# A fused two-block network on one core: GpSimd takes the lower halves of sixteen weight tiles

## What is computed

```
mod   = (silu(c)     @ w_mod[l] + b_mod[l])
mod_c = (silu(c_ctx) @ w_mod[l] + b_mod[l])
...
hc = modulate(ctx_s, g_norm1[l], csh1, csc1)
zc = hc @ w_in[l]
qc, kc, vc = qkv_heads(zc, g_q[l], g_k[l])
...
yc_attn = gqa(qc, kc, vc)
yc_conv, yc_four = local_branches(zc, w_conv[l])
ctx_s = ctx_s + cgt1 * merge_branches(zc, yc_conv, yc_four, yc_attn, ...)
```

## Time and profile before

| what | value |
|---|---|
| median of 3 runs | 3247.83 us (3245.22 to 3250.43) |
| the profiled execution | 3244.21 us |
| its span in the trace | 3242.4 us |
| mean granted TensorE clock | 0.991 of full speed |
| context attention with its 52 tiles | about 89 to 224 us of the span |

### The profile page before, as it was taken

One profiled execution on the slowest core, in us unless ns is written; L12 is line 12 of the kernel. 1 busy time (PEld: TensorE's weight loads), 2 busy tenths in 40 slices (PEclk: granted clock), 3 DMA queues, 4 the chain that ended last, 5 costly groups with the idle time before them and its releaser, 6 DMA issues.

```text
span 3242.4 us, 42575 instructions
## 1 busy us (share of the span) xinstructions
PE 3180.1 (98%) x16062; PEld 2675.1 (83%) x16062; DVE 2084.7 (64%) x2904; ACT 1232.2 (38%) x1792; POOL 0.2 (0%) x4
## 2 busy tenths in 40 slices
PE   8899999999999999999999999999999999999998
PEld 6889998887888888888788888887888878888886
DVE  6777886665687777656475565875544676664446
ACT  4664445454232223554332222535222266542221
POOL 0000000000000000000000000000000000000000
PEclk9999999999999999999999999999999999999999
DMA  7654552212344553311222322222222336223232
GB/s 272 202 187 158 179 190 85 72 53 72 110 137 140 175 186 104 104 52 53 82 88 91 103 97 97 79 97 78 98 97 96 106 72 88 69 78 104 98 97 72
DMA packets 100715, 358.17 MB, mean 110 GB/s; under 512 B 11208, under 2 KB 12368, under 8 KB 100560
## 3 DMA queue, kind: packets, MB, share of 16 engines
q1 hardware_dynamic: 98864, 352.85, 32.8%
q10 hardware_dynamic: 1696, 3.16, 2.1%
HBM read 351.76 MB, written 2.10 MB: 109 GB/s over the span
## 4 chain that ended last, share of the span: by engine, by line
PE 90%; DVE 5%; ACT 2%; issue 1%; DMA 0%; DVEq 0%; ACTq 0%; SPq 0%
PE ring L1689 26%; PE ring L1690 25%; PE ring L1691 25%; PE bank L1689 2%; PE bank L1691 2%; PE bank L1690 2%; DVE w_lo L2580 1%; ACT w_hi L898 1%; PE ring L2015 1%; PE ring L2016 1%; PE bank L2040 1%; PE bank L2041 1%; PE ring L1986 1%; DVE x L3340 0%; PE bank L2171 0%
## 5 line engine op out<-in xcount | busy, mean ns | idle before, releaser
L1689 PE MATMUL ring<-h_hi,w_hi 128*128 128x512 f32 (+1 forms) x2776 | 1027.2, 370 | 18.2 <-DVE h_lo L2651 8.4
L1690 PE MATMUL ring<-h_lo,w_hi 128*128 128x512 f32 (+1 forms) x2776 | 1019.2, 367 | 0.0
L1691 PE MATMUL ring<-h_hi,w_lo 128*128 128x512 f32 (+1 forms) x2776 | 1019.0, 367 | 0.0
L2580 DVE TENSOR_TENSOR w_lo<-raw,w_hi 128x1024 fp32r<-128x1024 f32 x598 | 730.9, 1224 | 306.6 <-ACT w_hi L898 293.9
L898 ACT ACTIVATE w_hi<-raw 128x1024 fp32r<-128x1024 f32 x598 | 630.5, 1056 | 707.5 <-PE ring L1691 667.7
L1689 PEld LDWEIGHTS ring<-h_hi,w_hi 128*128 128x128 f32 x2776 | 528.7, 190 | 111.4 <-issue 16.3
L1691 PEld LDWEIGHTS ring<-h_hi,w_lo 128*128 128x128 f32 x2776 | 528.1, 190 | 86.1
L1690 PEld LDWEIGHTS ring<-h_lo,w_hi 128*128 128x128 f32 x2776 | 528.7, 190 | 82.3
L1689 PE MATMUL ring<-y_hi,w_hi 128*128 128x512 f32 (+1 forms) x1456 | 540.2, 371 | 11.5 <-DVE z L2870 7.8
L1691 PE MATMUL ring<-y_hi,w_lo 128*128 128x512 f32 (+1 forms) x1456 | 536.4, 368 | 0.0
L1690 PE MATMUL ring<-y_lo,w_hi 128*128 128x512 f32 (+1 forms) x1456 | 536.2, 368 | 0.0
(11 more groups left out here) (381 smaller groups left out, 3075.1 us busy)
## 6 DMA issues: line engine op xcount, KB each, us to landing
raw<-ws SPq DMA_DIRECT2D x606, 512.0 KB, 3.3
z<-ws SPq DMA_DIRECT2D x52, 512.0 KB, 4.5
x<-ws SPq DMA_DIRECT2D x4, 512.0 KB, 9.5
x<-x_t SPq DMA_DIRECT2D x1, 2048.0 KB, 10.9
out_t<-x SPq DMA_DIRECT2D x8, 256.0 KB, 2.0
z<-xc ACTq DMA_DIRECT2D x6, 256.0 KB, 11.3
xc<-ctx_t SPq DMA_DIRECT2D x1, 1024.0 KB, 12.4
z<-ropes ACTq DMA_DIRECT2D x2, 512.0 KB, 4.0
```

The source lines that it names most:

```text
L1689: nc.tensor.matmul(o, a_hi, b_hi, start=start, stop=False)
L1690: nc.tensor.matmul(o, a_hi, b_lo, start=False, stop=False)
L1691: return nc.tensor.matmul(o, a_lo, b_hi, start=False, stop=stop)
L2580: nc.vector.tensor_tensor(w_lo[:, u, :], raw[:, u, :], f(w_hi[:, u, :]), ALU.subtract).then_inc(w_ready, 1)
```

## The change

The lower part of every second modulation tile (odd index i, the second of each pair) of this attention is computed by GpSimd: 16 tiles, numbers 2, 5, 8, 11, 15, 18, 21, 24, 28, 31, 34, 37, 41, 44, 47 and 50. GpSimd waits for `w_hi_ready` of the tile, subtracts, and raises its own count `s_pool_low`. GpSimd does not raise `w_ready`. VectorE does that: when it comes to its next call of `lower_w`, it first waits for its own earlier tiles, then for GpSimd, and raises `w_ready` by one; then it makes the tile of that call. The loads, ScalarE's queue and TensorE's queue are unchanged.

```diff
+POOL_MODS = (1,)
...
+        pool_tiles = [at0 + n for kind, layer, stream, at0 in steps if (kind, layer, stream) == ("attn", 0, "ctx")
+                      for n, (of, i) in enumerate(fill_tiles(layer, stream)) if of == "mod" and i % 2 in POOL_MODS]
...
+        @block.gpsimd
+        def _(pool):
+            for n, t in enumerate(pool_tiles):
+                pool.wait_ge(w_hi_ready, t + 1)
+                nc.gpsimd.tensor_tensor(w_lo[:, t % R, :], raw[:, t % R, :], w_hi[:, t % R, :].bitcast(F32), ALU.subtract)\
+                    .then_inc(s_pool_low, 1)
...
+            pool_read = [0]
+
             def lower_w(c, off=0):
 
                 t = c + LEAD
                 if isinstance(off, int) and t >= n_tiles:
+                    return
+                while pool_read[0] < len(pool_tiles) and pool_tiles[pool_read[0]] < t:
+                    dve.wait_ge(w_ready, pool_tiles[pool_read[0]])
+                    pool_read[0] += 1
+                    dve.wait_ge(s_pool_low, pool_read[0])
+                    dve.sem_inc(w_ready, 1)
+                if t in pool_tiles:
                     return
```

More of the change, by code:

```diff
@@ L588, in build @@
         s_chunk_sum = sem("mod_products_summed")
+        s_pool_low = sem("w_lo_ready_by_pool")
         s_out = sem("stored")
```

## The result

The changed kernel takes 3253.1 us (median of 20 runs, 3250.2 to 3256.7), the kernel before 3247.5 us in the same rounds: a ratio of 1.0018, 95% interval 1.0012 to 1.0025. One of the 20 executions of the kernel before took 16463 us and is left out of the ratio. The changed kernel is slower by 5.6 us, where +2 was forecast and +7.5 was the price of the rival in which GpSimd and VectorE shut each other out. The time lies in the range given and inside the band called "same", near its upper end.

A forecast was written before the change was run, and what follows sets the result against it. TensorE, busy 98%, was taken to bound the kernel, VectorE counting only where TensorE waits for it. Terms +1.5 + 1.3 + 1.3 - 2.15 gave +2 us on 3247.8: 3250 us, range 3244 to 3258 us.

The forecast's parts named there:

- the case in which the engines run side by side: Context attention: GpSimd and VectorE work without blocking each other; +2 us, 3250 us, 48% chance.
- the shut-out: Rival: GpSimd's subtraction and VectorE's operations on two local-memory operands cannot run together; +7.5 us, 3255 us, 25% chance.
- What bounds the kernel: Context attention: TensorE is busy 98% of the span; freeing VectorE is worth only TensorE's waits for it, 11.7 us.
- d = 2.45 us: GpSimd's time for one subtraction of 1024 columns, taken as twice VectorE's 1.226 us.
- The relief, -2.15 us: Tiles 15, 28 and 41, directly before branch reads: reads come earlier by 0.45, 1.0 and 0.7 us.
- the rival of the relief: Rival: TensorE's waits at three branches go, 5.6 us, plus 1.5 us of half clock; -7 us, 3241 us, 10% chance.
- The first chain, +1.5 us: Tiles 8 and 9, before the query parts and TensorE's longest single wait: 1.3 us later, plus hand-overs.
- The second chain, +1.3 us: Tile 50, before the load of tile 54 and TensorE's last wait: 1.1 us later, plus the hand-over.
- The other ten pairs, +1.3 us: Remaining odd tiles and the tiles behind them: mostly covered, 1.3 us together, mostly at tiles 21 to 25.
- my three terms: The added delays at tiles 8 and 9, at tile 50 and at the other ten pairs: +1.5, +1.3 and +1.3 us.
- the rival with a slow GpSimd: Rival: a GpSimd subtraction takes near 4.9 us or starts several us late; some +17 us, 3265 us, 7% chance.
- the half clock forecast at 151 to 157 us: Changed profile: a stretch of half clock there would speak for GpSimd and VectorE excluding each other.

The follow-up runs named there:

- e7: Changed kernel with all 16 lower parts left out, made by nobody, VectorE passing readiness on itself: 3242.5 us, 0.9986 of the kernel before.
- e12: Changed kernel with only the lower parts of tiles 15, 28 and 41 left out and GpSimd doing nothing: 3242.4 us, 0.9987 of the kernel before.
- e2: Changed kernel with tiles 8 and 50 back on VectorE, so GpSimd makes 14: 3252.3 us, 1.0020 of the kernel before.
- e3: Changed kernel with GpSimd filling the 16 lower parts with zeros twice (2.0 us) instead of subtracting, all waits kept: 3244.8 us, 0.9996 of the kernel before.
- e10: Changed kernel with GpSimd filling the 16 lower parts with zeros three times (3.0 us) instead of subtracting, waits kept: 3252.4 us, 1.0013 of the kernel before.
- e8: The changed kernel unaltered, timed again and traced a second time: 3252.7 us, 1.0022 of the kernel before.
- e11: Changed kernel with GpSimd only filling tiles 15, 28 and 41 with zeros, twice, instead of subtracting: 3241.6 us, 0.9981 of the kernel before.
- e9: Changed kernel with only TensorE and SyncE waiting for GpSimd, which subtracts in two instructions of 512 columns: 3251.7 us, 1.0018 of the kernel before.

## Why the prediction came out as it did

The forecast was the case in which the engines run side by side, and that case is wrong. The time fell in the range because the range had been stretched over the shut-out, and that it came within 3 us of the forecast is luck. By its steps:

- **What bounds the kernel**: right. Only VectorE's work in front of a branch read or the query parts matters; e7 and e12 show that thirteen of the sixteen subtractions were worth nothing that the times or traces can tell.
- **d = 2.45 us**: measured 2.40 us (2.35 to 2.80). By the Trainium skill's ratio of 1.96 (GPSIMD Engine Reference, section Performance versus the Vector engine) it would be an estimated 2.40 us: the trace agrees.
- **The relief, -2.15 us**: mis-sized, about -4 us by e12 and e7. The idle time was right, the half clock behind the wait at 186 us was left out of the term and put only into the rival of the relief.
- **The first chain, +1.5 us**: TensorE's wait for L2865 went from 3.4 to 5.0 and 4.8 us, +1.6 and +1.4. Right in the size of the wait; that it costs as much of the whole time is not shown, since e2 takes it back and is not faster.
- **The second chain, +1.3 us**: failed. TensorE's wait there went from 2.7 to 2.6 us, because the load behind tile 50 took 3.17 us instead of 4.38. I had taken the load's length as fixed; why it is shorter is not shown.
- **The other ten pairs, +1.3 us**: the waits alone, e3 against e7, cost 0.10% at 2.0 us and e10 another 0.17% at 3.0 us. At 2.4 us all waits together are thus about 5 us over the relief (0.03 + 0.14%), against 4.1 us in my three terms. Roughly right, and the agreement is within the intervals. The slope measured between 2.0 and 3.0 us, 5.5 us for one more microsecond, lies between the 3.4 us of my three terms (4.1 us for 1.22 us) and the 7 us of the rival with a slow GpSimd (17 us for 2.45 us); it has the casts of e10 in it.
- **The shut-out**, in the prediction a rival with 25%: this is the step that failed, the assumption that a GpSimd instruction leaves VectorE's alone. Its mechanism is much as described: a softmax part (L2923) at the first branch and L2894 at the second and third wait out GpSimd, and the convolution of the front is held up by tile 2 (L2846, 2.63 us), which makes TensorE wait 0.7 us at 93 us. Around tiles 21 to 25 TensorE has new waits of 0.5 us and of 2.5 us in the first trace, 0.4 us in e8; the half clock forecast at 151 to 157 us is in the first trace, from 151.4 to 154.8 us, and not in e8. It adds an estimated 5 to 6 us to a kernel that without it would stand at about +1 us. The rival's price of +7.5 was 2 us too high: it put 2.5 us on the first chain, where the wait grew by 1.6 and 1.4, and 1.3 us on the second, where it did not grow. It also named only operations on two operands; casts are shut out as well.
- The rule of the Trainium skill (SBUF — State Buffer, section Who interferes with whom) that GpSimd and a VectorE operation with two inputs in local memory exclude each other for the whole instruction: by that rule, the traces agree, with the stretches of 1.3 to 2.2 us and the undisturbed L2891. Its other condition for such operations, that GpSimd must read to be in the way, agrees too: the fills of e3, e10 and e11 stretch none of them. For casts that condition does not hold: e10's fills stretch five.

The parts are relief -4, waits +5, shut-out +5 to 6, together +6 to +7, for +5.6 in the first rounds and 0.22%, 7 us, in those of e8. This sum is no proof, since the shut-out's part was got as the rest.

## What to carry to other kernels

Work moved from VectorE to GpSimd is not taken off VectorE if both work on local memory: a two-input VectorE instruction beside a GpSimd subtraction stands still, and a cast beside any GpSimd work seen here. So 1.2 us saved can be 2.2 us lost somewhere else in the queue, here 12.9 us lost of 19.6 us saved, and some of it at a worse place. Before moving work off an engine, leave it out altogether for one run: here that run (4 us for all sixteen, and the same for three) shows the most that any such move could have won. And where the receiving engine's result is passed on by the first engine's next step, everything between is late by what the receiving engine needs longer, here 1.2 us.

## What was not expected of the hardware

- A cast is shut out as well. L2864 copies 64 x 256 numbers with one input in local memory and took 2.40 us instead of 0.29, from 180.01 to 182.41, beside GpSimd's subtraction from 179.85 to 182.25. For a cast a fill is enough: in e10 it took 1.00 us beside one.
- In the changed kernel the instruction that begins first runs through, so at 148 us a difference of 0.2 us decides which VectorE instruction is lengthened, and it differs between executions. In e9 a GpSimd instruction that stood ready was passed by VectorE's next one.
- Splitting GpSimd's subtraction in two made it slower, 3.85 us at most against 2.8, since it loses its turn in the middle (e9).
- A fill of 128 x 1024 numbers takes GpSimd 0.95 us and leaves VectorE's two-input instructions at their usual length, 0.42 us for an L2865.
- The half clock behind a wait of 3.4 to 3.7 us lasted 3 us in one trace of the kernel before and 10 us in another.
